# Second gate product, bonus, values and normalisation in other places; ScalarE alone copies queries and keys out of PSUM

## What is computed

```python
mix = concat([mla(p), rwkv7(p), short_conv(p)])      # p = h @ w_in
h = LN(ALPHA*h + mix @ w_out)
h = LN(ALPHA*h + hier_moe(h))                        # 2 of 32 experts for each token

# attention: q, k of 64 values without position and 32 rotated, 8 heads, causal softmax
# rwkv7, four heads of 64:
g = sigmoid(xg) @ w_gate_out
S, y = scan(S*diag(w) - kk^T(a*kk) S + v k^T, y = S r)     # chunks of 64 tokens in the kernel
m = mean(y); var = mean((y - m)**2)
yn = (y - m)*rsqrt(var + GN_EPS)*lnx_g + lnx_b
bonus = sum(r*k*r_k)*v
out = (yn + bonus)*g
```

## Time and profile before

| | |
|---|---|
| median of three runs | 3286.67 us (3281.77 to 3293.94) |
| profiled execution | 3302.33 us, its span 3300.5 us |
| PE busy | 2812.4 us, 85% |
| DVE busy | 1449.4 us, 44% |
| ACT busy | 775.9 us, 24% |
| POOL busy | 654.2 us, 20% |
| mean granted clock of TensorE | 0.907 |

### The profile page before, as it was taken

How to read it: one execution, slowest core, us unless ns; L and a number is a source line. 1 busy time by engine, 2 the same in 40 slices (tenths; PEclk the granted TensorE clock), 3 DMA queues, 4 the chain that set the end, 5 groups by cost and what they waited for, 6 DMA issues and landing times.

```text
span 3300.5 us, 56743 instructions
## 1 busy us (share of the span) xinstructions
PE 2812.4 (85%) x22522; PEld 1582.4 (48%) x22522; DVE 1449.4 (44%) x4004; ACT 775.9 (24%) x1847; POOL 654.2 (20%) x651
## 2 busy tenths in 40 slices
PE   6998888888888969999499978888888799599990
PEld 3545666666654533333145456666666555233330
DVE  4112666665553362222451056666655434422227
ACT  0101344444441100111100023444444221011111
POOL 1000111111100015555310010111101000355534
PEclk9997888989998979999699968899999899799995
DMA  7113222322213347998641132332222314499956
GB/s 270 61 38 92 90 86 86 87 87 86 86 35 133 115 187 281 358 365 314 251 163 49 39 109 71 102 93 87 84 66 77 131 65 183 161 360 361 363 185 236
DMA packets 171844, 503.08 MB, mean 152 GB/s; under 512 B 48413, under 2 KB 89377, under 8 KB 146369
## 3 DMA queue, kind: packets, MB, share of 16 engines
q1 hardware_dynamic: 101760, 307.91, 27.1%
q0 software_dynamic: 50240, 120.23, 10.7%
q10 hardware_dynamic: 19584, 71.31, 5.5%
HBM read 629.93 MB, written 86.89 MB: 217 GB/s over the span
## 4 chain that ended last, share of the span: by engine, by line
PE 76%; DVE 10%; ACT 4%; issue 3%; DMA 3%; DVEq 3%; another core or an unknown queue 1%; POOL 0%; ACTq 0%; SPq 0%; POOLq 0%
PE ps L812 68%; PE ps L809 8%; DMA c_x<-xd 2%; DVE grams L2174 1%; DVE S_all L2622 1%; ACT PT L1651 1%; ACT S_all L1902 1%; DVE c_x L2210 1%; DMA c_b<-ybd,dga 1%; ACT kT L1651 0%; DVEq L2623 0%; DVE negm L2624 0%; ACT tokm L1651 0%; DVE c_h L2188 0%
## 5 line engine op out<-in xcount | busy, mean ns | idle before, releaser
L812 PE MATMUL ps<-w_slots,xbT 128*64 128x512 f32 (+1 forms) x2048 | 460.0, 602 | 18.5 <-DVE xbT L3097 18.5
L812 PE MATMUL ps<-hT,w_in 128*128 128x512 f32 x896 | 391.4, 598 | 3.3 <-ACT hT L1651 3.3
L739 POOL DMA_INDIRECT xb<-xd,idall x256 | 257.0, 1004 | 152.7 <-issue 81.0
L812 PEld LDWEIGHTS ps<-w_slots,xbT 128*64 128x64 f32 x2048 | 144.2, 138 | 289.0 <-issue 269.8
L812 PE MATMUL ps<-w_out,o_mixT 128*128 128x512 f32 x576 | 261.5, 602 | 19.3 <-issue 18.0
L812 PEld LDWEIGHTS ps<-hT,w_in 128*128 128x128 f32 x896 | 171.3, 192 | 216.6 <-issue 211.6
L812 PE MATMUL ps<-w_slots,hidT 128*64 128x512 f32 (+1 forms) x1024 | 233.5, 596 | 8.3 <-issue 7.1
L3097 DVE STREAM_TRANSPOSE xbT<-xb 128x1024 f32<-128x1024 f32 x64 | 79.7, 1245 | 321.2 <-DMA xb<-xd,idall 321.2
L812 PE MATMUL ps<-grams 64*64 64x64 f32 (+1 forms) x4624 | 181.1, 227 | 27.1 <-DVE grams L2174 16.6
L812 PEld LDWEIGHTS ps<-grams 64*64 64x64 f32 (+1 forms) x4624 | 160.5, 140 | 58.3 <-issue 31.7
L812 PE MATMUL ps<-kcat,qcat 96*128 96x512 f32 (+3 forms) x384 | 171.9, 561 | 8.6 <-DVE negm L2624 8.6
(11 more groups left out here) (388 smaller groups left out, 4383.6 us busy)
## 6 DMA issues: line engine op xcount, KB each, us to landing
w_slots<-in_w_gu SPq DMA_DIRECT2D x64, 2048.0 KB
w_slots<-in_w_dn SPq DMA_DIRECT2D x64, 1024.0 KB
ybd<-yb ACTq DMA_DIRECT2D x64, 512.0 KB
pd<-stage SPq DMA_DIRECT2D x56, 256.0 KB, 2.5
out_y<-c_h ACTq DMA_DIRECT2D x27, 512.0 KB, 2.9
w_in<-in_w_in SPq DMA_DIRECT2D x6, 2048.0 KB, 24.8
o_mixT<-mixd SPq DMA_DIRECT2D x18, 512.0 KB, 4.5
o_h<-out_y SPq DMA_DIRECT2D x18, 512.0 KB, 5.1
```

The lines of the kernel that those rows point to most:

```text
L739: pool.indirect_dma_start(xb[p % 2][:, 256 * q:256 * q + 256], None, x_quarters, bass.IndirectOffsetOnAxis(ap=idall[:, NE * q + p:NE * q + ...
L812: return pe.matmul(out, lhsT, rhs, start=start, stop=stop, skip_group_check=True)
```

## The change

- A second place for the gate. The gate buffer is chosen by tile: `gate` for even tiles, part of `vrow` for odd ones, and `wlora` for tile 7. At a seam the product goes to `K[1]` instead of `K[2]` and waits for `st1` instead of `y`; ACT copies it as the first step of the slot. `kks` takes over the wait for `y`, `kn` waits for the gate's copy, and `tokm` no longer does.
- ACT copies both halves of the queries and of the keys in slots 1 to 7. DVE's `qn` and `kn` are gone there, with the waits on them. In the first slot and the sample tile they stay.
- A new step `z` on DVE forms bonus times values plus the bias row, in `mix`, behind `off3` of its own tile. `yn` keeps four of its six products. `y` and `hnx` use `uu` and `u2` instead of two parts of `grams`.
- In a slot DVE does `hnx` after the mask of head 4 instead of head 2, and `yn` after `rr0` instead of before `gramD`. `rkv` is cut in two around the mask of head 3. `mixT` stands before `sq1` instead of before `gramD`, on PE and ACT, and `sq1` waits for ACT's copy of it.
- PE and ACT do some transposes, `kn` and `V` in another order among the attention steps.

```diff
+        gate_of = [wlora[:] if i == NPT - 1 else vrow[:, 7, 0:256] if i % 2 else gate[:] for i in range(NPT)] + [gate_s]
@@ PE: gate, kks, kn, tokm, gramD, sq, mixT
                     if self.seam:
-                        pe.wait_ge(dve_a.sem, dve_a.at(("a", self.l, self.i - 1), "y"))
-                    self.done(mm(K[2][:W, 0:256], sg[:, :W], wgate[:], True, True), step)
+                        pe.wait_ge(dve_a.sem, dve_a.at(("a", self.l, self.i - 1), "st1"))
+                    out = K[1] if self.seam else K[2]
+                    self.done(mm(out[:W, 0:256], sg[:, :W], wgate[:], True, True), step)
@@
-                    pe.wait_ge(act_a.sem, act_a.at(self.k, "mlaT"))
+                    pe.wait_ge(act_a.sem, act_a.at(self.k, "gate" if self.seam else "mlaT"))
@@
-                        pe.wait_ge(act_a.sem, act_a.at(self.k, "gate"))
                         pe.wait_ge(act_a.sem, act_a.at(self.k, "qrT"))
@@
-                    if self.seam:
-                        pe.wait_ge(act_a.sem, act_a.at(("a", self.l, self.i - 1), "mixT"))
                     self.done(self.gram(0, 1), "gramD")
@@
                 def sq(self, r):
                     W = self.W
+                    if r == 1 and self.seam:
+                        pe.wait_ge(act_a.sem, act_a.at(("a", self.l, self.i - 1), "mixT"))
@@
                     if self.i + 1 < NPT:
-                        pe.wait_ge(act_a.sem, act_a.at(("a", self.l, self.i + 1), "kn"))
-                        pe.wait_ge(dve_a.sem, dve_a.at(("a", self.l, self.i + 1), "kn"))
+                        pe.wait_ge(dve_a.sem, dve_a.at(("a", self.l, self.i + 1), "sq0"))
@@ PE: slot
+                t.pt(0, 0)
                 x.kn()
-                t.pt(0, 0)
                 t.pt(0, 1)
                 t.s(2)
+                x.V()
                 t.pt(1, 0)
                 t.pt(1, 1)
                 t.s(3)
-                x.V()
                 t.pv(0)
@@
                 t.s(4)
+                t.pt(3, 0)
                 x.tokm()
-                t.pt(3, 0)
-                w.mixT()
+                x.gramD()
                 t.pt(3, 1)
-                x.gramD()
                 t.s(5)
@@
                 t.s(7)
+                w.mixT()
                 x.sq(1)
@@ ACT: qn, kn
+                    if self.seam:
+                        cp(dst[0:64].rearrange("p (h two) t -> p h two t", two=2)[:, :, 1, :], v3(K[3], 4)[64:128])
@@
+                    if self.seam:
+                        cp(kcat[0:64].rearrange("p (h two) t -> p h two t", two=2)[:, :, 1, at:at + P], v3(K[1], 4)[64:128])
@@ ACT: slot
+                x.gate()
                 x.qn()
                 t.p(0)
                 x.exps()
+                t.pt(0, 0)
                 t.p(1)
-                t.pt(0, 0)
                 x.kn()
                 t.pt(0, 1)
+                t.pt(1, 0)
                 t.p(2)
-                t.pt(1, 0)
                 t.pt(1, 1)
+                x.V()
                 t.p(3)
-                x.V()
@@
                 t.p(4)
-                x.gate()
+                t.pt(3, 0)
                 x.tokm()
-                t.pt(3, 0)
-                w.mixT()
@@
                 t.p(7)
+                w.mixT()
                 x.sq(1)
@@ DVE
+                def z(self):
+                    W = self.W
+                    z2 = mix[:W]
+                    z4 = z2.rearrange("p (h v) -> p h v", h=RH)
+                    dve.wait_ge(act_a.sem, act_a.at(self.k, "mv"))
+                    tt(z4, tokm[:W, 0:2, :].rearrange("p f (a v) -> p (f a) v", a=2), bc(bon[:W], [W, RH, 64]), ALU.mult)
+                    dve.drain()
+                    self.done(tt(z2, z2, rows[:W, R_LXB:R_LXB + 256], ALU.add), "z")
@@ DVE: end_of_slot
                 x.off3()
+                x.z()
                 b.turned(0)
@@ DVE: slot
                 t.s(1)
-                x.qn()
                 x.qr()
                 t.s(2)
+                x.kk2()
+                x.rkv_begun()
+                t.s(3)
+                x.rkv_ended()
+                t.s(4)
                 w.hnx()
-                x.kk2()
-                x.kn()
-                t.s(3)
-                x.rkv()
-                t.s(4)
-                w.yn()
                 x.gramD()
@@
                 x.rr(0)
+                w.yn()
                 t.s(7)
```

More of the change, by code:

```diff
@@ L176 @@
 DVE_SATT = "r0 r1 s0 m0 T0 r2 s1 m1 r3 o0 T1 s2 m2 o1 T2 s3 m3 o2 T3 o3".split()
-PE_A = ("gramD gram23 sq0 gram4 rr0 sq1 rr1 sq2 rr2 off1 off2 mv off3 wt "
-        "u0 st0 u1 st1").split()
+PE_A = ("2gramD 2gram23 2sq0 2gram4 2rr0 1mixT 2sq1 2rr1 2sq2 2rr2 2off1 2off2 2mv 2off3 2wt "
+        "2u0 2st0 2u1 2st1").split()
 PE_S = ("q kkb qlat qrT tokm gramD gram23 new sq0 gram4 rr0 sq1 rr1 sq2 rr2 off1 off2 mv off3 wt").split()
@@ L202, in plan @@
 def plan(T):
-    heads = range(NH)
+    heads, three = range(NH), range(3)
     T["dve"].plan("init", ["zero", "idx"])
@@ L243, in plan @@
             if i:
-                T["pe_a"].plan(("a", l, i), PE_A)
-                T["act_a"].plan(("a", l, i), ACT_A)
-                T["dve_a"].plan(("a", l, i), DVE_A)
+                for n, own in (("pe_a", PE_A), ("act_a", ACT_A), ("dve_a", DVE_A)):
+                    for step in own:
+                        T[n].plan(("a", l, i - 1 if step[0] == "1" else i), [step[1:]])
             for n, seam in (("pe_a", PE_SEAM), ("act_a", ACT_SEAM), ("dve_a", DVE_SEAM), ("pool_a", POOL_SEAM)):
@@ L251, in plan @@
                         T[n].plan(("a", l, t), [step[1:]])
+            if j is None:
+                T["dve_a"].plan(("a", l, i), ["hnx", "yn"])
+                T["pe_a"].plan(("a", l, i), ["mixT"])
+                T["act_a"].plan(("a", l, i), ["mixT"])
         T["pe_s"].plan(("sfin", l), ["m", "wT", "oT", "a"])
@@ L260, in plan @@
                                                                       for h in heads], []) + ["R"])
-                T["act_b"].plan(("att", l, i - 1), ["p0"] + sum([([f"p{h + 1}"] if h + 1 < NH else []) + pts[h] for h in heads], []) + ["R"])
+                if i < NPT:
+                    begun = ["p0", "pt0.0", "p1"] + pts[0][1:] + ["pt1.0", "p2"] + pts[1][1:] + ["p3"] + pts[2]
+                else:
+                    begun = ["p0"] + sum([[f"p{h + 1}"] + pts[h] for h in three], [])
+                T["act_b"].plan(("att", l, i - 1), begun + sum([([f"p{h + 1}"] if h + 1 < NH else []) + pts[h] for h in range(3, NH)], []) + ["R"])
                 T["dve_b"].plan(("att", l, i - 1), [f"s{h}" for h in heads] + ["rden", "a"])
@@ L1797, in gate @@
                     if self.seam:
-                        act.wait_ge(dve_a.sem, dve_a.at(("a", self.l, self.i - 1), "yn"))
-                    self.done(cp((gate_s if self.sample else gate)[:W], K[2][:W, 0:256]), "gate")
+                        act.wait_ge(pe_a.sem, pe_a.at(self.k, "gate"))
+                    src = K[1] if self.seam else K[2]
+                    self.done(cp(gate_of[self.i][:W], src[:W, 0:256]), "gate")
                 def mlaT(self):
@@ L2580, in hnx @@
                     W = self.W
-                    y2, z2 = (v[:W] for v in ((yt_s, yt2_s) if self.sample else (yt, yt2)))
+                    y2, z2 = (v[:W] for v in ((yt_s, yt2_s) if self.sample else (uu, u2)))
                     y4, z4 = (v.rearrange("p (h v) -> p h v", h=RH) for v in (y2, z2))
@@ L2604, in yn @@
                     tt(y2, y2, rows[:W, R_LXG:R_LXG + 256], ALU.mult)
-                    tt(z2, z2, rows[:W, R_LXB:R_LXB + 256], ALU.add)
                     dve.drain()
-                    tt(y2, y2, z2, ALU.add)
+                    tt(y2, y2, mix[:W], ALU.add)
                     dve.drain()
                     dve.wait_ge(act_a.sem, act_a.at(self.k, "gate"))
-                    self.done(tt(mix[:W], y2, (gate_s if self.sample else gate)[:W], ALU.mult), "yn")
+                    self.done(tt(mix[:W], y2, gate_of[self.i][:W], ALU.mult), "yn")
             class Att:
```

45 lines of the change are left out of this document (28 added, 17 removed).

## The result

The changed kernel takes **3192.1 us** (median, 3191.7 to 3192.9) against 3290.3 (3281.8 to 3294.5) for the kernel before on the same chip: a ratio of 0.970, interval 0.968 to 0.973, **98 us less**. The forecast was 3214 and -73. The profiled executions are 3192.2 (span 3190.0) and 3302.3 (span 3300.5), 110 apart; the profile of before lay 12 above its median. What follows divides up the 110.

What follows compares the result with a forecast made beforehand. TensorE (76% of the span) bounds it, waiting in each slot's head on a chain mostly paced by VectorE. Head -134, tail +57, last slot -1.5, `xs` load +6 give -73: 3286.7 to 3214 us, range 3186 to 3262.

Steps and rivals of the forecast that it cites:

- the head's gain: Slot start to first Gram products: 10.4 us less in slots 1 to 4, 8.5 in 5 to 7; 134 in all.
- the tail's payback: Behind the masks: second squaring waits for `yn` and the copy of `mixT`, 4.05 us later a slot, 57 in all.
- the clock row behind `rr0`: Sign of being wrong: the granted clock behind `rr0`, in the tail of the slot, reads 0.5.
- the rival with all of the clock back: Head of slots 1 to 4: full clock gives 12.5 us each, 17 more in all, time 3192; chance 0.15.
- the bounds: Head gain in slots 1 to 4: 8.3 us at the old clock, 12.5 if the head keeps 2.4 GHz.
- The walk to the turned queries: Slot 3's head followed step by step: turned queries go at 571.4 instead of 574.89, 3.5 us earlier.
- the clock drops in the tail: Rival: clock falls in the gap behind `rr0`, 2.5 us a slot, 35 in all, time 3249; chance 0.20.
- `z` at nothing: Two products behind `off3` cost nothing, as VectorE waits about 1.5 us there; uncovered, 12 us.
- `hnx` covered, with 0.8 to spare: Between head 4's mask and the Gram masks, `hnx` (2.3 us) is hidden beside transposes and Gram products.
- The load of `xs`: Next tile's load, issued behind the store after `mixT`, stalls `tanh` in slots 2 and 3: 3 us a layer, 6 in all.
- The rival built on it, 3309: Slower: `tanh` waits for `xs`, each us of landing beyond 8.6 costing one in 12 slots; 3309 at 17 us; chance 0.05.
- Outside the slots: In the last slot the two `z` products leave the path to the output product: 1.5 us gained.

Runs made afterwards that it cites:

- the kernel before with products in its head: Kernel before, with 128x128 products put into TensorE's two long idle stretches ahead of the turned queries and the token transposes: 3267.3 us, ratio 0.991.
- the late `mixT`: Changed kernel with `yn` and `mixT` put later in the slot: 3210.8 us; with the store of `mixC` also behind the next tile's loads: 3130.8 us.

## Why the prediction was right, and where it wasn't

The range held the time, and the mechanism, the head's gain less the tail's payback, is what the timelines show. But one of its own signs of being wrong came true, the clock row behind `rr0` reads 0.50. And that the rival with all of the clock back names the measured time, 3192, is luck: it had 151 for the head and 57 for the tail, and they measure 171 and 69. In the terms of the sum:

- **Head, -134 forecast, -171 measured.** The step that failed is the clock. For slots 1 to 4 I took 10.4, the middle of the bounds; they measure 13.0, a little above the upper one (12.5). The walk to the turned queries was right (3.5 earlier, measured 4.2 in slot 3); from there to the Gram products it had 7.2 us and the trace has 4.2, because each step runs at 2.4 GHz. Slots 5 to 7 measure 11.2 and not 8.5: I let slot 7 stand for all, which kept its clock for most of its head. Slots 5 and 6 of before did not: 11.9 and 3.4 us at 1.2 GHz in layer 0's heads, 9.3 and 13.2 in layer 1's. I had read no clock row there.
- **What made the head shorter.** Up to Gram, in 12 slots, and taken in this order: normalisation and gate 85, order of the values and exponentials 47, copies 10. My text gave the order half a sentence; it is a third of the gain. VectorE's two copies last 1.4 a slot, and 19 in 14 slots is the same; but only 10 of it in 12 slots lie up to Gram, and the rest came with the clock behind, so the agreement is in part luck.
- **Tail, +57 forecast, +69 measured.** The second step that was off: I counted 4.05 us of idle time a slot and no clock. The runs give 2.5 to 3.0 of idle time (35 to 40 us) and 1.5 to 1.8 of clock (21 us by the times). Idle, the term was too high: in slot 3 the second squaring moved from 0.73 to 4.36 behind the start of `rr0`, 3.6 where I had 4.2, and TensorE's idle stretches there are 3.1. The clock, which I priced apart at 2.5 a slot and 35 in all, was too high as well, but it belonged in the sum.
- **Two rivals at once.** "All of the clock comes back" and "the clock drops in the tail" stood as alternatives, with 0.15 and 0.20. Both are true, in different places of a slot, and they offset each other in part. They should have been combined.
- **The tail's clock, and the rule.** The new gap is the broken one that no row had shown, and the clock fell behind it in every slot: 0.50 from 565 to 571. The Trainium skill (TensorE: Matmul & The Clock Gate, Part 4: PE-mode transpose) says that transposes don't count as activity as matmuls do. The fall alone would agree; but a gap filled up with transposes kept the clock in 11 of 12 slots, so for this kernel the measurement speaks against the rule (it shows a clock that was held on transposes; no run shows one that rose on them). In this gap the clock did what the rule predicts; the cause it names is not the one that these runs support.
- **`z` at nothing:** right, with 0.65 us to spare, less than the 1.5 I had assumed.
- **`hnx` covered, with 0.8 to spare:** wrong by a little. It holds back the Gram masks, and they the first squaring. Slot 3 after, its first Gram products being at 553.09:

```profile
554.84 0.17 DVE L2620 TENSOR_SCALAR gn<-gn 128x4 f32<-128x4 f32 x1
554.92 1.27 DVE L2191 TENSOR_TENSOR grams<-ps,cst 128x128 f32<-128x128 f32 x6
...
557.08 1.15 PE L820 MATMUL ps<-grams 64*64 64x64 f32 x32 [0.36 <-DVE grams L2191]
```

The squaring starts 4.0 behind the first Gram products. In the kernel before with products in its head, at the same full clock, it is 3.4:

```profile
576.10 0.46 PE L812 MATMUL ps<-l,ta 64*64 64x64 f32 x16 [1.32 <-ACT mixC L1659]
...
579.47 1.15 PE L812 MATMUL ps<-grams 64*64 64x64 f32 x32
```

So `hnx` costs some 0.6 in slot 3. The second column of the table, 71.3 after, is 59.2 in that kernel; how much of these 12 us is `hnx` and how much the new order isn't settled.

- **The load of `xs`, +6 forecast, 0 measured.** The changed kernel issues it 3.3 us behind the copy of `mixT` in slot 3 (565.97 to 569.30), where I had carried over 5.2, and 11.4 ahead of `tanh`. (The working itself came to stalls of 1.8 and 2.8, 4.6 a layer, and took 3 without saying why.) The rival built on it, 3309, didn't occur, yet its mechanism is real: with a tail that is a few us shorter, it took 59 us at `tanh` in 12 slots and turned a gain of 63 into a loss of 16 (by the ratios) to 19.
- **Outside the slots,** 1.5 forecast, some 8 measured; 4.6 of it lies ahead of slot 1, where the kernel before with its products also came 5.5 earlier. That kernel has nothing of the change, so the 4.6 needn't come from it.

## What to carry over

A step that moves out of an engine's critical stretch needs two costs where it lands: the idle time that it makes there, and the clock that this idle time takes from the next microseconds; put it where work of the same engine covers it, not where its result is first allowed. Price a part up to the end of the stretch that repeats, not up to the next step: the new order gave 30 or 47 us up to Gram, by what else waited there, and 47 or 50 over the whole slots. And when a path is shortened, look at what is queued behind the moved step on SyncE: the loads for the next tile had stood behind a store for no reason, which cost nothing before (no `tanh` waited), nothing in the changed kernel, and 80 us, with the clock that it took along, one step later (3210.8 against 3130.8).

## What the runs showed of the hardware

- TensorE's granted clock fell behind a stretch in which it idled for 1.84 and 1.28 us with 0.44 us of transposes between; it did so in all 12 slots (2.8 to 3.1 us idle in each). With 128x128 products in that stretch it stayed at 1.00 in 12 slots, with transposes in 11.
- 58 us at 1.2 GHz behind the Gram products of 12 slots cost 22 us. Ahead of them, in the kernel before, products took 121 us at 1.2 GHz down to 31, and the time by 31.
- The next tile's rows, which wait for two small cache stores, were issued 1.6 us behind them in slot 3 of the changed kernel (1.6 to 1.9 in 11 of its 12 slots, 3.4 in one) and 5.5 us behind them where the gather into `S_all` was issued 0.2 us ahead. With the late `mixT` it was over 5 us in 7 of the 8 slots 1 to 4, where the gather goes out within 1 us of the stores, and 1.6 to 3.5 in slots 5 and 6, where it comes 1.7 us behind them or more. But in the kernel before it was up to 4.1 with the gather over 10 us away. That the gather is the cause is argued from the order of the lines; no run changed it alone.
